# The head norm's twelve statistics as a high and a low product

## The reference

```python
    S_new, o = retention_scan(qf, kf, vf, ret_state.astype(jnp.float32))
    o = o * lax.rsqrt(jnp.mean(o * o, axis=-1, keepdims=True) + EPS)
    o = o.reshape(B, T, RET_V_WIDTH).astype(xn.dtype)
    b_out = (jax.nn.silu(g) * o) @ w_ret_out

    merged = jax.nn.sigmoid(gate_a) * a_out + jax.nn.sigmoid(gate_b) * b_out
    return merged @ w_o, new_buf, S_new
```

## Time and profile before

| | |
|---|---|
| three runs | 1497.29, 1497.30 and 1497.96 us, median 1497.3 |
| profiled execution, first to last instruction (span) | 1495.6 us |
| TensorE matmul busy | 1475.2 us, 99% of the span |
| VectorE, GpSimd, ScalarE busy | 1001.0, 842.0 and 635.4 us |
| the 24 records of L1194 (two for each statistic) | 8.9 us busy, 452 ns each |
| pair 0's statistics, first and last start | 476.99 and 542.95 us |
| pair 1's statistics, first and last start | 641.61 and 661.82 us |

### The profile page before, as it was taken

How to read it: one execution, slowest core, us unless ns; L and a number is a source line. 1 busy time by engine, 2 the same in 40 slices (tenths; PEclk the granted TensorE clock), 3 DMA queues, 4 the chain that set the end, 5 groups by cost and what they waited for, 6 DMA issues and landing times.

```text
span 1495.6 us, 28307 instructions
## 1 busy us (share of the span) xinstructions
PE 1475.2 (99%) x11336; PEld 1455.2 (97%) x11336; DVE 1001.0 (67%) x1251; ACT 635.4 (42%) x929; POOL 842.0 (56%) x571
## 2 busy tenths in 40 slices
PE   8999999999999999999999999999999999999996
PEld 5999999999999999999999999999999999999995
DVE  7999888856545724576715876766657765574847
ACT  5533444344544541131213855556556332332333
POOL 3377776777545653257565445555555655554555
PEclk9999999999999999999999999999999999999998
DMA  6013333322356258621421144566759575454634
GB/s 217 22 42 94 114 114 113 113 80 65 112 176 205 75 200 296 219 80 50 149 78 50 29 149 171 199 237 219 253 193 326 203 285 189 142 208 156 227 107 170
DMA packets 110091, 229.13 MB, mean 153 GB/s; under 512 B 8960, under 2 KB 20992, under 8 KB 108304
## 3 DMA queue, kind: packets, MB, share of 16 engines
q1 hardware_dynamic: 95296, 204.30, 39.7%
q10 hardware_dynamic: 14672, 23.09, 4.6%
HBM read 154.41 MB, written 72.95 MB: 152 GB/s over the span
## 4 chain that ended last, share of the span: by engine, by line
PE 96%; POOL 1%; DMA 1%; ACT 1%; issue 1%; DVE 0%; POOLq 0%; SPq 0%; DVEq 0%; ACTq 0%
PE ps L1476 40%; PE ps L1237 26%; PE ps L1026 16%; PE ps L1402 3%; PE ps L1389 3%; PE ps L1074 2%; PE ps L1164 1%; PE ps L1169 1%; PE ps L1180 1%; PE ps L1166 1%; DMA cva_h<-conv_scratch 1%; PE ps L1147 0%; PE ps L1152 0%; PE ps L1194 0%; POOL w_l L931 0%
## 5 line engine op out<-in xcount | busy, mean ns | idle before, releaser
L1476 PE MATMUL ps<-tx_h,w_h 128*128 128x258 f32 x960 | 271.5, 283 | 0.0
L1476 PE MATMUL ps<-tx_l,w_h 128*128 128x258 f32 x960 | 271.3, 283 | 0.0
L1476 PE MATMUL ps<-tx_h,w_l 128*128 128x258 f32 x960 | 271.1, 282 | 0.0
L996 POOL TENSOR_TENSOR w_l<-raw,w_h 128x512 fp32r<-128x512 f32 x120 | 185.6, 1551 | 147.6 <-ACT w_h L2033 147.1
L1476 PE MATMUL ps<-fx_l,w_h 128*128 128x258 f32 x720 | 203.7, 283 | 0.0
L1476 PE MATMUL ps<-fx_h,w_h 128*128 128x258 f32 x720 | 203.6, 283 | 0.0
L1476 PE MATMUL ps<-fx_h,w_l 128*128 128x258 f32 x720 | 203.4, 282 | 0.0
L1476 PEld LDWEIGHTS ps<-tx_h,w_h 128*128 128x128 f32 x960 | 181.4, 189 | 0.1
L1476 PEld LDWEIGHTS ps<-tx_l,w_h 128*128 128x128 f32 x960 | 181.4, 189 | 0.1
L1476 PEld LDWEIGHTS ps<-tx_h,w_l 128*128 128x128 f32 x960 | 181.2, 189 | 0.0
L2328 DVE SCALAR_TENSOR_TENSOR ps<-u_ext,wdw,ps 128x512 f32<-128x512 f32 x232 | 155.2, 749 | 0.0
(11 more groups left out here) (386 smaller groups left out, 4305.4 us busy)
## 6 DMA issues: line engine op xcount, KB each, us to landing
raw<-wseq_dram SPq DMA_DIRECT2D x260, 256.0 KB, 3.1
quad_scratch<-quad_h SPq DMA_DIRECT2D x16, 774.0 KB, 3.5
tx_h<-quad_scratch SPq DMA_DIRECT2D x12, 1032.0 KB, 10.4
tx_l<-hidden_scratch SPq DMA_DIRECT2D x12, 1032.0 KB, 12.8
gate_scratch<-gst SPq DMA_DIRECT2D x10, 1032.0 KB, 5.0
hidden_scratch<-hq_g SPq DMA_DIRECT2D x8, 1032.0 KB, 7.0
hidden_scratch<-stg_b SPq DMA_DIRECT2D x6, 1032.0 KB, 6.9
hq_g<-hidden_scratch SPq DMA_DIRECT2D x6, 1032.0 KB, 13.1
```

Of the source, the lines that this page charges most:

```text
L996: pool.tensor_tensor(lo, src, hi.bitcast(F32), ALU.subtract).then_inc(q_lo, 1)
L1476: out = pe.matmul(ps[:, 2 * n + s, 0:HC], RINGS[q % RING][wa][:, kk * P:(kk + 1) * P], OPS[x][xb][:, QK * kh + kk, at_:at_ + HC], start=(i ...
```

## The change

The sum of squares is split as other operands are: ScalarE copies it to fp32r (`osq_h`, in the place of the second half of the squares), VectorE subtracts the copy from it (`osq_l`, in the place of the first half), and TensorE multiplies the ones, read as fp32r, with the high and with the low part into the same bank. Two new semaphores carry it (`on_hi`, `on_lo`); two old ones are merged into others with their thresholds moved (`x0_sq` into `x_sq`, `hist_ld` into `wdw_ld`). In pair 0 the tables move some steps by a turn. In pair 1 the order is written out.

```diff
-NORM_SUM = {21: 0, 26: 1, 30: 2, 33: 3, 40: 4, 43: 5}
-NORM_STAT = {23: 0, 27: 1, 31: 2, 34: 3, 41: 4, 44: 5}
-NORM_SCALE = {26: 0, 29: 1, 33: 2, 35: 3, 42: 4, 45: 5}
+NORM_SUM = {21: 0, 25: 1, 29: 2, 33: 3, 40: 4, 43: 5}
+NORM_LO = {22: 0, 26: 1, 30: 2, 34: 3, 41: 4, 44: 5}
+NORM_STAT = {23: 0, 27: 1, 31: 2, 35: 3, 42: 4, 45: 5}
+NORM_SCALE = {25: 0, 29: 1, 33: 2, 36: 3, 43: 4, 46: 5}
...
             def out_stat(p, i):
-                pe.wait_ge(on_ad, 6 * p + i + 1)
+                pe.wait_ge(on_lo, 6 * p + i + 1)
...
-                pe.matmul(ps[:, 6 + i % 2, 0:CH], ones[:], osq[p * (i % 2)][:, 0:CH],
-                          start=True, stop=True).then_inc(on_st, 1)
+                k = p * (i % 2)
+                pe.matmul(ps[:, 6 + i % 2, 0:CH], ones[:].bitcast(F32R), osq_h[k][:], start=True, stop=False)
+                pe.matmul(ps[:, 6 + i % 2, 0:CH], ones[:].bitcast(F32R), osq_l[k][:], start=False, stop=True
+                          ).then_inc(on_st, 1)
...
+            def square_hi(p, i):
+                k = p * (i % 2)
+                act.wait_ge(on_ad, 6 * p + i + 1)
+                act.activation(osq_h[k][:], osq[k][:, 0:CH], ACT.Copy).then_inc(on_hi, 1)
...
+                if x in NORM_SUM:
+                    square_hi(0, NORM_SUM[x])
                 if x in NORM_STAT:
                     norm_root(0, NORM_STAT[x])
...
             norm_square(1, 1)
+            square_hi(1, 0)
             for i in range(2 * CHUNKS):
+                if i + 1 < 2 * CHUNKS:
+                    square_hi(1, i + 1)
                 norm_root(1, i)
...
+            def square_lo(p, i):
+                k = p * (i % 2)
+                dve.wait_ge(on_hi, 6 * p + i + 1)
+                dve.tensor_tensor(osq_l[k][:], osq[k][:, 0:CH], osq_h[k][:].bitcast(F32), ALU.subtract
+                                  ).then_inc(on_lo, 1)
...
             square_sum(1, 1)
+            square_lo(1, 0)
+            square_lo(1, 1)
             head_norm(1, 0)
             decode_state(1, DEC - 1)
             square_sum(1, 2)
             product_gate(0)
+            square_lo(1, 2)
             head_norm(1, 1)
             square_sum(1, 3)
             head_norm(1, 2)
+            square_lo(1, 3)
             product_gate(1)
             square_sum(1, 4)
             head_norm(1, 3)
+            square_lo(1, 4)
             square_sum(1, 5)
             head_norm(1, 4)
+            square_lo(1, 5)
             product_gate(2)
```

More of the change, by code:

```diff
@@ L249, in build @@
         osq = [place("osq0", [P, 2 * CH], F32, a_KT)[0], place("osq1", [P, 2 * CH], F32, a_PB)[0]]
+        osq_l = [place("osq_l0", [P, CH], F32R, a_KT)[0], place("osq_l1", [P, CH], F32R, a_PB)[0]]
+        osq_h = [place("osq_h0", [P, CH], F32R, a_KT + 4 * CH)[0], place("osq_h1", [P, CH], F32R, a_PB + 4 * CH)[0]]
         qk, vv = [qk0, qk1], [v0, v1]
@@ L271, in build @@
         x2_ld = sem("x2_ld")
-        x0_sq = sem("x0_sq")
         u_mm = sem("u_mm")
@@ L277, in build @@
         wdw_ld = sem("wdw_ld")
-        hist_ld = sem("hist_ld")
         piece_ld = [sem(f"piece_ld{i}") for i in range(4)]
@@ L349, in build @@
         on_ad = sem("on_ad")
+        on_hi = sem("on_hi")
+        on_lo = sem("on_lo")
         on_st = sem("on_st")
@@ L611, in _ @@
             sp.dma_start(x_in[:, :, 2 * CH:T], xT[:, :, 2 * CH:T]).then_inc(x2_ld, 16)
-            sp.dma_start(hist[:], cacheT).then_inc(hist_ld, 16)
+            sp.dma_start(hist[:], cacheT).then_inc(wdw_ld, 16)
             for n in range(2 * RAW, 16):
@@ L1595, in _ @@
             for i in range(4):
-                x_square(0, 2 * i, 2 * i + 2, xa_in[i], x0_sq)
+                x_square(0, 2 * i, 2 * i + 2, xa_in[i], x_sq)
             x_square(1, 0, 4, xb_in[0], x_sq)
@@ L2244, in square_half @@
                 if c:
-                    dve.wait_ge(x_sq, 2 * c + half - 1)
+                    dve.wait_ge(x_sq, 2 * c + half + 3)
                 else:
-                    dve.wait_ge(x0_sq, 2 * half + 2)
+                    dve.wait_ge(x_sq, 2 * half + 2)
                 return dve.tensor_tensor(q[:, a:a + 2], q[:, a:a + 2], q[:, a + 2:a + 4], ALU.add)
@@ L2343, in taps @@
                     n -= took
-            dve.wait_ge(wdw_ld, 48)
-            dve.wait_ge(hist_ld, 16)
+            dve.wait_ge(wdw_ld, 64)
             def u_out(j):
@@ L2566, in unit_turn @@
                     square_sum(0, NORM_SUM[x])
+                if x in NORM_LO:
+                    square_lo(0, NORM_LO[x])
                 if (v, j) in ROPE:
```

## The result

The changed kernel takes 1500.14 us (median of 20 runs, 1499.34 to 1500.93) against 1497.34 for the kernel before (20 runs on the same chip): ratio 1.0019, 95% interval 1.0012 to 1.0025, that is 2.8 us slower. The forecast was 1499.7. The profiled execution has a span of 1497.8 us, before 1495.6; its own time was 1499.8.

What follows compares the result with a forecast made beforehand. TensorE's own sequence was taken to set the end. Span 1495.6 + 2.8 (second pair) - 0.4 (first pair) = 1498.0, plus 1.7 for the runs' median: 1499.7 us, likeliest range 1498.9 to 1500.3, wider 1496.5 to 1501.2.

Steps and rivals of the forecast that it cites:

- Rival (6): In the statistics, the two halves cost a plain product each, 7 us more, so 1504 and later; chance 0.02.
- First pair: 0.4 forecast: First pair saves 1.6 us but meets the cva_h loads, so 0.4 us is gained, bounds 0 and 1.6.
- I find each low part ready by the time of its product: First pair: no low part delays its statistic; the tightest, statistic 2, has 0.7 us to spare.
- the landing moves with that trigger: End of first pair: cva_h lands according to its load trigger, not TensorE; trigger 0.6 us earlier, or 0.3.
- Second pair: +2.8 forecast: Second pair: VectorE with ScalarE sets the time; waits of 4.4 us less 1.6 given back, 2.8 us later.
- the waits may fall elsewhere and the end stay: Second pair: as VectorE with ScalarE sets the time, TensorE's 4.4 us of waits may move without moving the end.
- the decode state behind it waits for its own load and loses only 0.2: Second pair, VectorE behind the first head norm: norm starts at 645.1 instead of 643.43, decode state loses only 0.2 us.
- rival (5): Second pair: TensorE's clock falls in the new waits, 2 to 3 us of that giving 1502 or so; chance 0.03.
- signs of being wrong: TensorE's second-pair waits under 2 us in all, a clock dip, or products of the first pair waiting too.
- signs named ahead: Statistics of 0.31 us; second-pair waits 1.8 (first), 1.5 (fourth); product gate 2.8 us later; cva_h wait over 1 us.
- Rival (3): Both pairs: every wait is covered and 3.2 us come through, 1494.1; decided at second pair's statistic 0; chance 0.05.
- rival (4): L951 gets ahead of second pair's low part 2, or cva_h's trigger comes no earlier: 1500.6, up to 1501.5; chance 0.14.

Runs made afterwards that it cites:

- copy of 0 first: Changed kernel with, in the second pair, ScalarE's copy 0 ahead of the second square and VectorE's low part 0 ahead of the second sum: 1499.76 us, 1.0014 of before.
- second pair alone: Changed kernel with high and low parts only in the second pair, the first pair and its turns as before: 1501.24 us, 1.0025 of before.
- filled kernel: Changed kernel with ten useless products ahead of statistic 0 and six ahead of statistic 2 of the second pair: 1500.41 us, 1.0019 of before.
- reordered kernel: Changed kernel with the second pair's ScalarE and VectorE work in another order, same instructions: 1498.61 us, 1.0006 of before.
- reordered again: Reordered kernel with square and sum of 4 ahead of root and norm of 3, low part of 4 ahead of the sum of 5: 1495.61 us.
- first-pair kernels: Changed kernel with only the first pair split, the second multiplying plain sums: 1497.19 us; with cva_h loads ahead of cva_l's first two: 1496.88 us.

## Why the prediction was right, and where it wasn't

**What a statistic gives back** came as worked out. From TensorE's timeline in the first pair, the two halves of statistic 0, 0.16 us apart, and the unit product behind them:

```profile
476.87 0.32 PE L1198 MATMUL ps<-osq_h,ones 128*128 128x344 f32 x1
477.03 0.32 PE L1199 MATMUL ps<-osq_l,ones 128*128 128x344 f32 x1
477.84 0.36 PE L1242 MATMUL ps<-sx_h,wx_h 128*128 128x258 f32 x1 [0.48 <-DVE v L2515]
```

Rival (6) is out.

**First pair: 0.4 forecast, 1.39 in the two traces (1.27 of it in A, 0.12 ahead of statistic 0), 0.16 in the medians.** Two steps failed. "I find each low part ready by the time of its product" was true and not enough: I looked at the statistic's product alone. The decode copy stands behind low part 0 and the rotary products on VectorE, and the unit products wait for it; the third row above is due at 477.18 and, with its slower restart, loses 0.7. So six statistics save 1.6 and 0.9 is left, as A shows between kernels whose loads landed in time (158.46 to 157.58). And "the landing moves with that trigger": the trigger didn't come 0.3 to 0.6 earlier but 0.08 later than in the earlier trace rows, and `cva_h` was there all the same. The trigger on SP's timeline, and then the landing from the view of the tile `cva_h`:

```profile
545.74 0.33 SPq L638 DMA_DIRECT2D raw<-wseq_dram  x1
```

```profile
DMA to landing us min/median/max: 5.5/6.7/7.9
```

In the trace of before the median landing took 8.9 us from its issue, in the kernel with the copy of 0 first 9.0, with triggers from 545.7 to 546.0. The second pair alone, whose first pair is that of before, landed them in 6.7 and has an A of 158.46, 0.39 less than before. So of the 1.39 us some 0.4 is one execution's transfers. Where they took 9.0, TensorE waited and A was 159.05: nothing passed. The 0.4 lies between these ends, by luck as much as by its working; the step took the landing for fixed against its trigger, and it moves by over 2 us from one execution to the next.

**Second pair: +2.8 forecast, +3.65 in the traces.** The mechanism is the one foreseen: statistic 0 late by its order on ScalarE, VectorE and ScalarE from then on ahead of TensorE in the chain, the product gate of set 3 letting group 5 go. For the sentence that "the waits may fall elsewhere and the end stay" the filled kernel is the evidence, with a wait of 1.06 at statistic 3 and the end 0.13 earlier; the copy-first kernel bears it out in part, since the wait went from statistic 0 to 2. By statistic, from when TensorE was due (the rows leave out about 0.15 of each wait), forecast and measured: statistic 0, 1.8 and 1.83; statistic 2, 0.15 and 1.16; statistic 3, 1.5 and none; statistic 5, 0.95 and 0.34. In place of the third stands the half-speed stretch. Its record gives 3.4 us, so 1.7 lost; 1.83 + 1.16 + 0.34 + 1.7 and 0.1 for each of three restarts make 5.3, less 1.6 gives 3.7.

The mis-sized step is "the decode state behind it waits for its own load and loses only 0.2". It lost 1.2: it ended 12.55 us into the pair, before 11.36. It didn't start much later (10.10 us in, before 9.95, where it waited for its load), but GpSimd's two pieces did: they wait for the decode products behind statistic 0, and so came 9.10 us in, before 7.44, and ran beside the decode state. Before, they had ended by then. VectorE's wait and GpSimd's timeline before:

```profile
DVE v_bc L2489 <- DMA v_bc<-v_sample_scratch: 1.4, 1, 1.4
```

```profile
643.28 1.04 POOL L850 TENSOR_TENSOR w_h<-raw,zero 128x512 fp32r<-128x512 f32 x1 [4.39 <-PE ps L1180]
644.39 1.30 POOL L853 TENSOR_TENSOR w_l<-raw,w_h 128x512 fp32r<-128x512 f32 x1
```

VectorE's timeline in the changed kernel, and then GpSimd's:

```profile
644.55 1.66 DVE L2504 TENSOR_SCALAR v_bc<-v_bc,qk 128x256 f32<-128x256 f32 x2
...
648.27 0.52 DVE L2520 TENSOR_TENSOR osq<-osq 128x344 f32<-128x344 f32 x1 [1.27 <-ACT osq L1755]
...
651.12 1.93 DVE L2520 TENSOR_TENSOR osq<-osq 128x344 f32<-128x344 f32 x1
```

```profile
643.55 1.04 POOL L853 TENSOR_TENSOR w_h<-raw,zero 128x512 fp32r<-128x512 f32 x1 [6.12 <-PE ps L1183]
644.67 1.38 POOL L856 TENSOR_TENSOR w_l<-raw,w_h 128x512 fp32r<-128x512 f32 x1
...
650.08 2.60 POOL L954 TENSOR_TENSOR ma<-ma,bop_b 128x1032 f32<-128x1032 f32 x1 [4.03 <-DVE bop_b L2660]
```

The two instructions of L2504 take 0.60 together in the reordered kernel, where GpSimd had ended its pieces, and 1.66 here; square, sum and low part of 2 follow behind. The sum of 3 at 651.12 stood behind L954, as forecast. The Trainium skill's page "SBUF — State Buffer", "Who interferes with whom", says that issue order decides who stands still; the trace agrees for the sum, which came 1.04 us behind L954 and ended 0.37 behind it.

**The dip of rival (5).** I gave it 0.03, named a dip among the signs of being wrong, and it came, behind waits of 1.68 and 1.00 us. What failed is the price, 1502: I took 2 to 3 us without a row behind them, where 1.7 was lost, and added the loss to the waits, but where VectorE is the bound it only takes the place of the next wait (0.13 us by the filled kernel). The runs of the changed kernel point the same way: eleven have a mean granted clock of 0.995 and average 1500.33 us, four have 0.997 and average 1500.12. Where TensorE is the bound the loss does count (1.56 us in the reordered pair). The Trainium skill's page "TensorE: Matmul & The Clock Gate", Part 1, says that idleness lowers the clock and activity gives it back; filling the waits bears that out (0.52 from 652 to 655 with the waits empty, 1.00 with them filled).

**The sum** lies 0.4 us under the median and 0.1 under the profiled execution, through errors of opposite sign: 1.0 too little gained up to the second pair, 0.85 too little lost in it. That they cancel is luck. Of the signs named ahead, the 0.31 us of a statistic, the first wait and the late product gate (by 3.65 rather than 2.8) came; the waits at the fourth statistic and for `cva_h` didn't. Of the signs of being wrong two came: the dip, and a product of the first pair that waits (0.48 us, L1242). Rival (3) is out. Of rival (4) the first condition is out: the low part of 2 (649.91 to 650.42) was under way when L954 started at 650.08, and didn't stand still. Its second came true, since the trigger of `cva_h` came no earlier, but not its price, since the loads landed sooner.

## What to carry to other kernels

Work that is split off TensorE onto the engines that feed it is paid in their order: the same instructions cost 3.65 us in one order and gave 1.15 in another, so when such a change disappoints, follow the feeding engines' rows from the first late product before judging the idea. For each instruction put into an engine's queue, look at every one behind it and who waits for that, not only at its own consumer. And before removing a wait of TensorE, ask whether another engine's chain runs through the same place: then the wait may only move.

The best kernel here is the changed one, reordered again: 1495.61 us, 0.9988 of before (0.9979 to 0.9997), about 1.9 us faster.

## What the runs showed of the hardware that I had not expected

- The granted clock fell to its lower level behind single waits of 1.77 us (second pair alone), 2.06 (reordered) and 2.10 us (copy of 0 first), and in the changed kernel behind 1.68 and 1.00 us with 7 us of work between them, not behind the first. It stayed there for 3.4 us, in the copy-first kernel for 6.8. Ten and six products, or twelve, in place of the idle time kept it up. Single waits of up to 1.06 us left it at 1.00. (At the start of the span it also stands at 1.00 through 5.7 us without a product; what ran before isn't in the trace.)
- The same four loads of `cva_h`, issued at the same place, landed in 6.7 to 9.0 us (medians of one execution each, in ten kernels), while the DMA engines moved 396 GB/s at 550 to 552 us in the changed kernel and 301 in the one before, at shares of 1.02 and 0.93. What makes the difference stays open, and so does what else spreads the runs of the first-pair kernels over 1.4 to 1.9 us.
